# RWKV recurrence in a one-core kernel: the triangular inverse of each chunk built from 32x32 tiles, with X and U packed in 32 columns

## The reference, cut to what matters

```python
def rwkv_step(S, inp):
    r_t, w_t, k_t, v_t, kk_t, a_t = inp
    sa = jnp.einsum('dbhij,dbhj->dbhi', S, -kk_t)
    S = (S * w_t[..., None, :] + sa[..., :, None] * (kk_t * a_t)[..., None, :]
         + v_t[..., :, None] * k_t[..., None, :])
    y = jnp.einsum('dbhij,dbhj->dbhi', S, r_t)
    return S, y
...
    S0 = jnp.zeros((2, B, RWKV_HEADS, HEAD_DIM, HEAD_DIM), jnp.float32)
    _, ys = lax.scan(rwkv_step, S0, xs)
```

## Time and profile before

| | us |
|---|---|
| median of 3 runs | 2685.48 |
| lowest, highest | 2685.13, 2686.86 |
| the profiled execution | 2688.1 |
| its span, first to last instruction | 2686.8 |
| TensorE busy | 2487.4 (93%) |
| VectorE, ScalarE, GpSimd busy | 1454.7, 928.5, 220.6 |
| mean granted TensorE clock | 0.965 |
| the recurrence, 1828 to 2190 us | 362 |

### The profile page before, as it was taken

How to read it: one execution, slowest core, us unless ns; L and a number is a source line. 1 busy time by engine, 2 the same in 40 slices (tenths; PEclk the granted TensorE clock), 3 DMA queues, 4 the chain that set the end, 5 groups by cost and what they waited for, 6 DMA issues and landing times. The chain is left out here.

```text
span 2686.8 us, 42434 instructions
## 1 busy us (share of the span) xinstructions
PE 2487.4 (93%) x18244; PEld 1866.7 (69%) x18244; DVE 1454.7 (54%) x1943; ACT 928.5 (35%) x1248; POOL 220.6 (8%) x190
## 2 busy tenths in 40 slices
PE   8989999999999999999999999998777778979996
PEld 6767878888876667778888878776666656733332
DVE  6776446454558765455454566655675746421112
ACT  4454233232332243243232343345354333421111
POOL 1002010000010000010000010001110100133331
PEclk9989999999999999999999999999789888989998
DMA  4223322222234422232222235242111133489994
GB/s 176 85 75 118 110 79 94 94 94 94 94 112 124 127 94 82 75 107 97 94 94 94 94 128 194 97 157 69 24 32 25 21 107 126 161 327 378 396 381 177
DMA packets 100569, 343.28 MB, mean 128 GB/s; under 512 B 41376, under 2 KB 49952, under 8 KB 66592
## 3 DMA queue, kind: packets, MB, share of 16 engines
q1 hardware_dynamic: 86560, 332.13, 35.5%
q0 software_dynamic: 13824, 8.44, 1.0%
HBM read 368.29 MB, written 30.93 MB: 149 GB/s over the span
## 5 line engine op out<-in xcount | busy, mean ns | idle before, releaser
L566 PE MATMUL bank<-xg_hi,w_hi 128*128 128x512 f32 x1504 | 597.3, 397 | 12.0 <-DVE xg_lo L588 12.0
L566 PE MATMUL bank<-xg_hi,w_lo 128*128 128x512 f32 x1504 | 586.1, 390 | 0.0
L566 PE MATMUL bank<-xg_lo,w_hi 128*128 128x512 f32 x1504 | 585.9, 390 | 0.0
L553 DVE TENSOR_TENSOR w_lo<-w_raw,w_hi 128x2048 fp32r<-128x2048 f32 x165 | 378.7, 2296 | 193.5 <-ACT w_hi L549 193.4
L549 ACT ACTIVATE w_hi<-w_raw 128x2048 fp32r<-128x2048 f32 x165 | 314.3, 1905 | 248.6 <-PE bank L566 219.2
L566 PEld LDWEIGHTS bank<-xg_hi,w_hi 128*128 128x128 f32 x1504 | 282.7, 188 | 78.2 <-DVE w_lo L553 12.0
L566 PEld LDWEIGHTS bank<-xg_lo,w_hi 128*128 128x128 f32 x1504 | 282.8, 188 | 63.8 <-issue 6.0
L566 PEld LDWEIGHTS bank<-xg_hi,w_lo 128*128 128x128 f32 x1504 | 282.6, 188 | 59.6
L566 PE MATMUL bank<-f_h_hi,w_hi 128*128 128x512 f32 x384 | 151.3, 394 | 0.0
L566 PE MATMUL bank<-f_h_hi,w_lo 128*128 128x512 f32 x384 | 150.5, 392 | 0.0
L566 PE MATMUL bank<-f_h_lo,w_hi 128*128 128x512 f32 x384 | 149.0, 388 | 0.0
(11 more groups left out here) (491 smaller groups left out, 4309.8 us busy)
## 6 DMA issues: line engine op xcount, KB each, us to landing
w_raw<-stream SPq DMA_DIRECT2D x165, 1024.0 KB, 4.9
e_over_ring<-expert_rows SPq DMA_DIRECT2D x70, 1024.0 KB, 8.2
e_w_raw<-expert_rows SPq DMA_DIRECT2D x26, 1024.0 KB
p_spill<-p_stage SPq DMA_DIRECT2D x36, 256.0 KB, 2.3
na_bias<-bias_na SPq DMA_DIRECT2D x32, 160.0 KB, 4.7
mix_gate<-p_spill SPq DMA_DIRECT2D x16, 256.0 KB, 2.8
e_w_raw<-y_rows SPq DMA_DIRECT2D x8, 512.0 KB, 7.2
rw_rkv<-p_spill SPq DMA_DIRECT2D x12, 256.0 KB, 5.1
```

The source lines that it names most:

```text
L553: V.tensor_tensor(ring(m)["lo"][m % SLOTS][:, :], ring(m)["raw"][m % RAW][:, :], ring(m)["hi"][m % SLOTS][:, :].bitcast(F32), ALU.subtract ...
L566: return T.matmul(out_ap, lhsT, rhs, start=first, stop=last, skip_group_check=True)
```

## The change

Levels 1 to 4 no longer compute whole 64x64 products. A level `l` < 5 only couples entries inside the same 32x32 diagonal block, so `X` and `U` hold 32 columns for each matrix (`near`), and each matrix is worked as two tiles `g` of 32 rows by 32 columns. Of these only the 16 columns that the level changes are computed (`kept`). So every 64x64 matmul with 64 columns becomes two of 32x32 with 16: per (quarter, direction) the three products of a level go from 16 to 32 matmuls each. `AB` goes from 16 to 32 matmuls in the same way; `BA` keeps 16, with 32 columns. At level 5 (`far_u_product`, `far_xt_product`) there stay 16 and 16 matmuls, now 32x32 with 32 columns. `products("BL", ...)` and everything else on TensorE is unchanged. The `LT` x `X` product now waits for `X` of the level before, and the wait for `XT` moves ahead of the products with `U`. The copies of ScalarE and VectorE shrink: `U` from 512 columns to 128 (256 at level 5), `X` from 512 to 128, `XT` from 512 to 256; level 0 in two halves from 256 to 64 (`X`) and 128 (`XT`). There is one new mask tile, `rw_near_masks`, filled by four VectorE casts while the gate logits are computed.

```diff
             T.wait_ge(*by_dve.at("B", t))
-            products("AB", A_, B, by_dve, "X0", 1)
+            b = [take_bank(T, ("AB", t, d, q), by_dve, "X0", t, q) for q in range(2)]
+            for i in range(4):
+                for g in range(2):
+                    for q in range(2):
+                        for e in range(2):
+                            rows, c = half_rows(q ^ e), (2 * i + e) * HEAD + g * NEAR
+                            mm = matmul(T, b[q][near_rows(1 - e, g), i * FEW:(i + 1) * FEW], A_[rows, c:c + NEAR],
+                                        kept(B[rows, c:c + NEAR], 0, x_side)[:, :, 0])
...
                 if l == 1:
                     T.wait_ge(*by_act.at("LT", t, 1))
                 else:
-                    T.wait_ge(*by_dve.at("XT", t, l - 1))
+                    T.wait_ge(*by_dve.at("X", t, l - 1))
                 for n in range(8):
                     for e in range(2):
-                        mm = block_product(b, n, 1 - e, e, one["LT"], one["X"])
+                        if l < LEVELS - 1:
+                            for g in range(2):
+                                mm = u_product(b, n, e, g, l)
+                        else:
+                            mm = far_u_product(b, n, e)
...
+                if l > 1:
+                    T.wait_ge(*by_dve.at("XT", t, l - 1))
                 T.wait_ge(*by_act.at("U", t, l))
...
                         if l < LEVELS - 1:
-                            mx = block_product(b_x, n, e, 1 - e, XT, one["U"])
-                        mm = block_product(b, n, e, e, one["U"], XT)
+                            for g in range(2):
+                                mx = x_product(b_x, n, e, g, l)
+                                mm = xt_product(b, n, e, g, l)
+                        else:
+                            mm = far_xt_product(b, n, e)
...
+            def x_product(b, n, e, g, l):
+                rows = near_rows(e, g)
+                o = b[near_rows(1 - e, g), n * FEW:(n + 1) * FEW].rearrange("p (b h) -> p b h", h=1 << l)
+                return matmul(T, o, XT[rows, n, near_cols(g)], kept(U[rows, n, :], l, x_side))
...
-                A.activation(one["U"][:, :, :], blocks(held("U", t, d, l), 8), ACT.Copy).then_inc(*done.mark("U", t, l))
+                if l < LEVELS - 1:
+                    A.activation(kept_of(near(one["U"]), l, up_low[d][1]), packed(held("U", t, d, l), 8, l, FEW),
+                                 ACT.Copy).then_inc(*done.mark("U", t, l))
...
-                V.copy_predicated(XT[:, :, :], repeated(rw_masks[:, 2 * l + up, :], 8),
-                                  blocks(held("XT", t, d, l), 8)).then_inc(*done.mark("XT", t, l))
+                V.copy_predicated(kept_of(XT[:, :, :], l, up), kept_mask(rw_masks, l, up, 8),
+                                  packed(held("XT", t, d, l), 8, l, HALF)).then_inc(*done.mark("XT", t, l))
```

More of the change, by code:

```diff
@@ L178, in _conv_taps @@
     return np.concatenate([rows.reshape(P, -1), same], axis=1)
+NEAR = 32
 def _level_masks():
@@ L1923, in dve_second @@
                     *dve_kk.mark("masks"))
+                of_level = rw_masks_f32.rearrange("p (m c) -> p m c", c=HEAD)
+                for g in range(4):
+                    rows, c = slice(NEAR * g, NEAR * (g + 1)), slice(NEAR * (g % 2), NEAR * (g % 2 + 1))
+                    V.tensor_copy(rw_near[rows, :, :], of_level[rows, 0:2 * (LEVELS - 1), c]).then_inc(
+                        *dve_kk.mark("near", g))
                 ts(V, rw_omka[:, :], vec[:, col["k_a"]:col["k_a"] + 4], -1.0, 1.0, ALU.mult, ALU.add).then_inc(
@@ L1991, in fours, with near, near_rows, near_cols @@
         return slice(4 * q, 4 * q + 4)
+    def near(m):
+        return m[:, :, 0:NEAR]
+    def near_rows(e, g):
+        return slice(e * CHUNK + g * NEAR, e * CHUNK + (g + 1) * NEAR)
+    def near_cols(g):
+        return slice(g * NEAR, (g + 1) * NEAR)
+    def kept(ap, l, side):
+        return ap.rearrange("p (b w h) -> p b w h", w=2, h=1 << l)[:, :, side]
+    def kept_of(ap, l, side):
+        return ap.rearrange("p n (b w h) -> p n b w h", w=2, h=1 << l)[:, :, :, side]
+    def kept_mask(mask, l, side, n):
+        one = kept(mask[:, 2 * l + side, :], l, side)
+        return one.unsqueeze(1).to_broadcast([P, n, one.shape[1], 1 << l])
+    def packed(b, n, l, width):
+        return b[:, 0:n * width].rearrange("p (n b h) -> p n b h", n=n, h=1 << l)
     def quad(b):
@@ L2137, in direction @@
             A_, B, K, Bh, Kh = [one[m][:, :] for m in ("A", "B", "K", "Bh", "Kh")]
-            XT = one["XT2"][:, t % 2]
+            XT, X, U = one["XT2"][:, t % 2], near(one["X"]), near(one["U"])
+            xt_side, x_side = up_low[d]
             yield from steps(1 + d)
@@ L2160, in products, with u_product @@
                             mm.then_inc(*done.mark(name, t, q))
-            def block_product(b, n, e, out_half, lhs, rhs):
-                return matmul(T, b[half_rows(out_half), n * HEAD:(n + 1) * HEAD], lhs[half_rows(e), n, :],
-                              rhs[half_rows(e), n, :])
-            T.wait_ge(*by_dve.at("B", t))
-            products("AB", A_, B, by_dve, "X0", 1)
-            products("BL", B, A_, by_act, "LT", 1)
-            products("BA", B, A_, by_dve, "XT0")
+            def u_product(b, n, e, g, l):
+                rows = near_rows(1 - e, g)
+                o = b[near_rows(e, g), n * FEW:(n + 1) * FEW].rearrange("p (b h) -> p b h", h=1 << l)
+                return matmul(T, o, one["LT"][rows, n, near_cols(g)], kept(X[rows, n, :], l, x_side))
@@ new lines, in x_product, with xt_product @@
+            def x_product(b, n, e, g, l):
+                rows = near_rows(e, g)
+                o = b[near_rows(1 - e, g), n * FEW:(n + 1) * FEW].rearrange("p (b h) -> p b h", h=1 << l)
+                return matmul(T, o, XT[rows, n, near_cols(g)], kept(U[rows, n, :], l, x_side))
+            def xt_product(b, n, e, g, l):
+                rows, c = near_rows(e, g), n * HALF + g * FEW
+                o = b[rows, c:c + FEW].rearrange("p (b h) -> p b h", h=1 << l)
+                return matmul(T, o, U[rows, n, :], kept(XT[rows, n, near_cols(g)], l, xt_side))
@@ new lines, in far_u_product, with far_xt_product @@
+            def far_u_product(b, n, e):
+                rows = near_rows(1 - e, x_side)
+                return matmul(T, b[near_rows(e, xt_side), n * NEAR:(n + 1) * NEAR],
+                              one["LT"][rows, n, near_cols(xt_side)], X[rows, n, :])
+            def far_xt_product(b, n, e):
+                rows = near_rows(e, xt_side)
+                return matmul(T, b[near_rows(e, x_side), n * NEAR:(n + 1) * NEAR], U[rows, n, :],
+                              XT[rows, n, near_cols(xt_side)])
@@ new lines, in direction @@
+            products("BL", B, A_, by_act, "LT", 1)
+            b = [take_bank(T, ("BA", t, d, q), by_dve, "XT0", t, q) for q in range(2)]
+            for i in range(4):
+                for q in range(2):
+                    for e in range(2):
+                        rows, c = half_rows(q ^ e), half_rows(2 * i + e)
+                        mm = matmul(T, b[q][half_rows(e), i * HALF:(i + 1) * HALF], B[rows, c],
+                                    kept(A_[rows, c], 0, xt_side)[:, :, 0])
+                    if i == 3:
+                        mm.then_inc(*done.mark("BA", t, q))
@@ L2348, in act_identities @@
             one, done = rw[d], act_rw[d]
-            A.activation(one["X"][:, :, :], repeated(rconst("ident2"), 8), ACT.Copy).then_inc(*done.mark("X", t))
+            A.activation(near(one["X"]), rconst("ident4").unsqueeze(1).to_broadcast([P, 8, NEAR]), ACT.Copy).then_inc(
+                *done.mark("X", t))
             if t >= 2:
@@ L2418, in direction @@
                 A.wait_ge(*by_pe.at("U", t, l))
-                A.activation(one["U"][:, :, :], blocks(held("U", t, d, l), 8), ACT.Copy).then_inc(*done.mark("U", t, l))
+                if l < LEVELS - 1:
+                    A.activation(kept_of(near(one["U"]), l, up_low[d][1]), packed(held("U", t, d, l), 8, l, FEW),
+                                 ACT.Copy).then_inc(*done.mark("U", t, l))
+                else:
+                    A.activation(near(one["U"]), held("U", t, d, l)[:, 0:8 * NEAR].rearrange("p (n c) -> p n c", n=8),
+                                 ACT.Copy).then_inc(*done.mark("U", t, l))
                 yield
@@ L2561, in direction @@
                 V.wait_ge(*by_act.at("XT", t))
[L2562 to L2563 removed]
+                V.copy_predicated(kept_of(near(one["X"])[:, fours(q), :], 0, low), kept_mask(rw_near, 0, low, 4),
+                                  packed(held("AB", t, d, q), 4, 0, FEW)).then_inc(*done.mark("X0", t, q))
             for q in range(2):
                 V.wait_ge(*by_pe.at("BA", t, q))
[L2566 to L2567 removed]
+                V.copy_predicated(kept_of(XT[:, fours(q), :], 0, up), kept_mask(rw_masks, 0, up, 4),
```

(1 more changed line is left out.)

14 lines of the change are left out of this document (7 added, 7 removed).

## The result

The changed kernel takes 2753.64 us (median of 4 runs, 2751.25 to 2754.43), the kernel before beside it 2685.31 us: ratio 1.0259, 95% interval 1.0247 to 1.0271. That is 68.3 us slower, where 54.8 were forecast; the time lies inside the range.

The account below looks back on a forecast made before the run. The prediction took the bringing of instructions to bound the dense parts up to level 4. Records +48.8, other waiting +6 and level 4 to `GA` 0 gave +54.8 us, so 2740 us, range 2712 to 2782.

Parts of the forecast that it names:

- The bound: Dense parts up to level 4: TensorE eats instructions faster than they are brought, 3.6 to 4.0 us a transfer.
- Records and transfers: Whole kernel: 3328 records more, 21572 in all; some 26 instruction transfers more, about 172 in all.
- The price: Stretches up to level 4: 29.5 ns a record (28.8 to 31.6), 211.8 us against 163.02, +48.8 us.
- The other waiting: Stretches up to level 4: of 22.6 us beyond the instructions, most vanishes beneath longer pacing; +6 us kept.
- the second rival: The rival (b): no waiting is absorbed and the clock falls, +91, 2777 us; chance 0.14.
- Level 4 to `GA`: Behind the dense stretches: shorter copies against level 4's added records, -2.6 to +1.9 us a quarter, taken as 0.
- Copies: Copies of 128 and 256 columns take about 0.30 and 0.44 us; in paced stretches their savings give nothing.
- The wait rule: `LT` x `X` waiting for `X` alone: worth nothing where instructions pace, up to 0.7 us at level 5.
- (a): Instructions do not pace, the engines' own work does: 49 us, about half on the path, -27, 2658 us; chance 0.11.
- (b): All 22.6 us of waiting remain and the falling clock costs 20: +91, 2777 us, up to 2800; chance 0.14.
- (c): Transfers in 3.4 us, 27.2 ns a record, and waits for `XT` go: +16, 2701 us; chance 0.06.
- (d): Whole kernel: gain and loss cancel within 5 us, 2685 us; chance 0.03.

Follow-up runs that it names:

- e10: Changed kernel with all 32 columns of each tile streamed in levels 1 to 4 instead of 16 (computes other values than the reference): 2750.32 us, ratio 1.0234.
- e6: Kernel before plus 3072 records: matmuls with the full 64x64 stationary and one moving column behind the three products of levels 1 to 4: 2784.65 us, ratio 1.0368.
- e8: Kernel before with B A and B R merged into one product, K A and K R too, 512 records less: 2675.24 us, ratio 0.9961.
- e12: Changed kernel with B A and B R merged into one product, K A and K R too, 512 records less: 2737.64 us, ratio 1.0188 to the kernel before.
- e1: Kernel before with an extra one-element matmul behind each of the three products of levels 1 to 4, 3072 records more: 3387.87 us, ratio 1.2617.
- e2: Kernel before with an extra one-element matmul behind the `LT` x `X` products of levels 1 to 4 only, 1024 records more: 2895.79 us, ratio 1.0790.
- e9: Kernel before with eight already fulfilled waits ahead of each matmul of levels 1 to 4, 6144 instructions more, no records: 3273.44 us, ratio 1.2186.
- e4: Kernel before with all matmuls in full, only the copies shrunk to the 32 kept columns (levels 0 to 4): 2679.37 us, ratio 0.9975.
- e5: Changed kernel with the old wait back, `LT` x `X` waiting for `XT` of the level before: 2756.23 us, ratio 1.0258 to the kernel before.
- e11: Kernel before with B A and B R merged, K A and K R too, and copies on the kept 32 columns alone: 2665.19 us, ratio 0.9916.
- e3: Kernel before with its 64x64 products, same count, streaming and copying only the 32 kept columns (levels 0 to 4): 2685.03 us, ratio 0.9993.
- e7: Kernel before with two one-element matmuls in each of 64 bursts of levels 1 to 4, 256 records more: 2703.22 us, ratio 1.0059.

## Why the prediction was right, and where its sum was off

**The bound.** Instructions pace the dense parts: shown for the changed kernel, by seven steps of 126 or 127 records at half clock with TensorE idle for a third of the time, and by e10, where twice the columns cost next to nothing. That it is their bringing rests on the match of these steps with the 16384-byte transfers; no run changed the bringing alone. For the price in general the evidence is weaker than I wanted: e6 bounds it from above (32 ns with the engine's own time in it), e8 and e12 gave about half of it where their records fell away, and e1, e2 and e9 measured something else.

**Records and transfers.** 21572 and 172, as counted.

**The price.** Forecast 29.5 ns; in the run of stalls 29.1. 7179 x 29.1 = 208.9 us.

**The other waiting: the term that was mis-sized.** Of 22.6 us I kept 6. Beyond 208.9 us the stretches hold 25.9, and they grew by 71.7 us where the sum had 54.8. The total of 68.3 came nearer to the forecast than that, by luck: stretches for which I had 0 or no term gave back 6.5 us. That all of it stayed, as the second rival had it, is right as a number and wrong as a picture: the wait for `XT` did vanish (20.4 to 4.0 us). One candidate for what took its place is matmuls that the change does not touch, at the lower clock. Groups of TensorE between the first `AB` and the last `GA`, before:

```profile
L566 PE MATMUL bank<-na_qk 64*128 64x512 f32 x56 | 17.3, 688 | 5.9 <-issue 5.9
L2324 PE MATMUL bank<-const_sb,na_score 128*128 128x128 f32 x96 | 14.5, 296 | 3.5 <-DVE rw_X L2588 2.0 <-issue 1.5
L566 PE MATMUL bank<-na_pT,na_v 128*64 128x256 f32 x96 | 11.9, 391 | 0.0
...
L566 PE MATMUL bank<-rw_R,rw_S 64*64 64x64 f32 x192 | 6.2, 220 | 0.0
```

and after:

```profile
L570 PE MATMUL bank<-na_qk 64*128 64x512 f32 x56 | 24.4, 963 | 0.0
L2404 PE MATMUL bank<-const_sb,na_score 128*128 128x128 f32 x96 | 20.8, 378 | 1.6 <-issue 0.7 <-DVE na_score L595 0.7
L570 PE MATMUL bank<-na_pT,na_v 128*64 128x256 f32 x96 | 17.3, 513 | 0.2 <-issue 0.2
...
L570 PE MATMUL bank<-rw_R,rw_S 64*64 64x64 f32 x192 | 9.0, 268 | 0.2 <-issue 0.2
```

These four alone went from 49.9 to 71.5 us busy. What the clock costs on the path is not 21.6, since part of it lies beside a transfer. The transfers in the four stretches came every 3.7 us or so where nothing else held them; what the intervals have beyond 3.7 us adds up to 22.2 us, and the longest is this:

```profile
1833.53 1.02 PE L570 MATMUL bank<-rw_A,rw_K 64*64 64x64 f32 x25
1836.63 1.34 PE L570 MATMUL bank<-rw_A,rw_K 64*64 64x64 f32 x39 [2.07 <-issue]
1837.90 2.08 PE L570 MATMUL bank<-na_qk 64*128 64x512 f32 x4
1839.90 1.97 PE L570 MATMUL bank<-rw_tok_V,rw_U 64*64 64x64 f32 x32
```

Between the transfers of 1833.62 and 1841.66 there are 96 records in 8.04 us, with 512-column matmuls of 0.5 us each. But the same sum of the intervals is 26.5 us in the kernel before, at a clock of 0.92 to 1.00, and 26.7 us in e10, at 0.69 to 0.77. So what comes on top of the transfers did not grow with the change, and from kernel to kernel it does not follow the clock: that the clock took the place of the waits is argued here and not shown. My sum had the clock in a rival only, though the earlier trace rows already showed 0.74 where TensorE was least busy; a term of its own would at least have been bounded. What part of the 17 us between forecast and result in the stretches the clock has, and what part is waiting for the S chain (13.2 us in the waits), no run has separated: none held the clock and changed nothing else.

**Level 4 to `GA`.** Forecast 0 in sum and within 3 us a quarter; it was -5.2 in sum. Three quarters gained 2.7, 2.7 and 6.0, the first lost 6.2, at a clock of 0.56 and with 27.53 of 30.56 us busy. The copies' gain was real (e4 has 8.0 us of it here); that the clock took some back in the first quarter fits its numbers, and was not tried apart. From `GA` to `AB` I had no term; it gave 4.4.

**Copies.** Forecast 0.30 and 0.44 us, measured 0.327 and 0.492 on average. The forecast holds for runs of four columns and more (0.28 to 0.30 and 0.42 to 0.43). Runs of two took 0.44 and 0.77 us, so the `XT` copy of level 1 got longer by the change; that runs of few columns could cost nothing either way was wrong for it. It did not show in the time, since the copies are off the path in the stretches, as argued: e4 gained nothing there.

**The wait rule.** Nothing, as e5 shows to within some 6 us.

**Rivals.** (a), the engines' own work, is out by e10 and by the stalls. (b) had the right second cause, but a larger price: it needs both full waits and 20 us for the clock. (c) needed 27.2 ns a record; it was 29.1. (d) is out by the ratio. Two slips in the sums change nothing: half of (a)'s 49 us is 25 and not 27, and the forecast's upper end stands as 2779 in the sum and as 2765 beside the chances.

## What to carry to other kernels

Before splitting matmuls into smaller tiles, count instructions per us in the stretch and look for stalls in the middle of a burst: where the count of records between such stalls is constant, each new record cost the same here however few columns it had, and merging products and shortening copies gave 22 us (e11) where packing the array cost 68. Bound what the granted clock can cost in a term of its own, for the untouched matmuls too: stretches with less streaming ran at a lower clock here, in the changed kernel and in e3 alike. Look at the length of the runs that a shortened copy leaves: with runs of two columns, half the columns took longer than all of them. And a filler that is to measure one thing must be tried against its own side effects: tile size and waits cost more here than what they were to measure.

## What the hardware showed that was not expected

- Changes between 64x64 tiles and those of a one-column stationary cost 0.18 to 0.20 us each in a row (e1, e2), 0.045 us between longer bursts (e7). The Trainium skill, "TensorEngine Tiling (Array Packing)", section Tiling Modes, says that a change of mode, unlike a change of tile, drains TensorE; the traces agree (the products of e2 beside such changes were busy for 225.0 us in place of 50.4), and the runs put these prices to it.
- An instruction of one or two long fulfilled waits ahead of a matmul cost TensorE 95 ns (e9: 586 us for 6144; 105 ns from one to the next in the trace).
- In e6, 74 records of `LT` x `X` on 64x64 tiles, of one or 64 columns, took 57 ns each at a granted clock of 0.50. In the changed kernel records of mostly 32x32 tiles at the same clock went at the pace of their instructions, 29.1 ns.
- Fewer columns with the same records went with TensorE busier, not less busy (e3: 35.76 against 30.12 us), and with a lower granted clock (0.75 against 0.91).
- A predicated copy of 256 columns in runs of two took 765 ns, in runs of 4 to 32 columns 420 to 428 ns, and one of 512 columns in one piece 716 ns.
